# Cross-attention of a two-block transformer layer: its scores and its weighted values as three fp32r products of rounded parts and remainders instead of one fp32 product

## The reference, cut to what matters

```python
def cross_attention(xn, memn, w_q, w_kv, w_o):
    q = (xn @ w_q).reshape(b, s, 4, 256)
    k, v = jnp.split(memn @ w_kv, 2, axis=-1)        # reshaped to 4 heads of 256
    scores = jnp.einsum('bqhd,bkhd->bhqk', q, k) * (256 ** -0.5)
    p = jax.nn.softmax(scores, axis=-1)
    o = jnp.einsum('bhqk,bkhd->bqhd', p, v).reshape(b, s, D_MODEL)
    return o @ w_o
```

## Time and profile before

| | |
|---|---|
| median of 3 runs | 2152.03 us (2150.19 to 2152.68) |
| span of the profiled execution, first to last instruction | 2149.0 us |
| PE busy | 2109.2 us, 98% of the span |
| DVE busy | 1218.3 us, 57% |
| ACT busy | 850.1 us, 40% |
| the query, attention and output stage | about 1670 to 1754 us of the span |

### The profile page before, as it was taken

How to read it: one execution, slowest core, us unless ns; L and a number is a source line. 1 busy time by engine, 2 the same in 40 slices (tenths; PEclk the granted TensorE clock), 3 DMA queues, 4 the chain that set the end, 5 groups by cost and what they waited for, 6 DMA issues and landing times. The chain is left out here.

```text
span 2149.0 us, 27234 instructions
## 1 busy us (share of the span) xinstructions
PE 2109.2 (98%) x10128; PEld 1709.0 (80%) x10128; DVE 1218.3 (57%) x1970; ACT 850.1 (40%) x1315; POOL 114.8 (5%) x117
## 2 busy tenths in 40 slices
PE   7999999999999999999999999999999999999998
PEld 7988888878777778878888887777777778888886
DVE  6886776755666445443333347778664454343443
ACT  7532222242344443342222236665775344232233
POOL 2000000022000000010000002000002000000001
PEclk9999999999999999999999999999999999999999
DMA  8655444534222224323333323112223212333332
GB/s 336 214 185 184 160 166 159 186 96 126 88 75 74 88 89 127 97 71 98 98 98 98 94 84 106 61 60 79 79 69 118 69 59 89 103 95 96 98 98 69
DMA packets 66777, 238.41 MB, mean 111 GB/s; under 512 B 7848, under 2 KB 10024, under 8 KB 65904
## 3 DMA queue, kind: packets, MB, share of 16 engines
q1 hardware_dynamic: 60768, 218.81, 31.7%
q0 software_dynamic: 3728, 16.08, 2.4%
q10 hardware_dynamic: 2176, 2.10, 0.3%
HBM read 230.12 MB, written 4.21 MB: 109 GB/s over the span
## 5 line engine op out<-in xcount | busy, mean ns | idle before, releaser
L2031 PE MATMUL bank<-hhi,whi 128*128 128x512 f32 x1504 | 595.0, 396 | 2.3 <-DVE wlo L1203 2.2
L2032 PE MATMUL bank<-hlo,whi 128*128 128x512 f32 x1504 | 586.0, 390 | 0.0
L2033 PE MATMUL bank<-hhi,wlo 128*128 128x512 f32 x1504 | 585.8, 389 | 0.0
L1203 DVE TENSOR_TENSOR wlo<-raw,whi 128x1024 fp32r<-128x1024 f32 (+1 forms) x352 | 428.7, 1218 | 273.1 <-ACT whi L595 270.5
L595 ACT ACTIVATE whi<-raw 128x1024 fp32r<-128x1024 f32 (+1 forms) x352 | 367.2, 1043 | 454.1 <-PE bank L2033 401.7
L2031 PE MATMUL bank<-ghi,whi 128*128 128x512 f32 (+1 forms) x936 | 358.8, 383 | 7.4 <-DVE glo L1212 4.4
L2032 PE MATMUL bank<-glo,whi 128*128 128x512 f32 (+1 forms) x936 | 355.2, 380 | 0.0
L2033 PE MATMUL bank<-ghi,wlo 128*128 128x512 f32 (+1 forms) x936 | 354.9, 379 | 0.0
L2031 PEld LDWEIGHTS bank<-hhi,whi 128*128 128x128 f32 x1504 | 282.4, 188 | 67.1 <-issue 6.2
L2033 PEld LDWEIGHTS bank<-hhi,wlo 128*128 128x128 f32 x1504 | 282.3, 188 | 60.1
L2032 PEld LDWEIGHTS bank<-hlo,whi 128*128 128x128 f32 x1504 | 282.6, 188 | 56.8 <-issue 0.7
(11 more groups left out here) (302 smaller groups left out, 1929.6 us busy)
## 6 DMA issues: line engine op xcount, KB each, us to landing
raw<-w SPq DMA_DIRECT2D x389, 512.0 KB, 3.6
work<-w SPq DMA_DIRECT2D x12, 512.0 KB, 11.2
raw<-w SPq DMA_DIRECT2D x16, 384.0 KB, 3.1
gated_in<-gated_in POOLq DMA_DIRECT2D x40, 64.0 KB, 1.9
gated_in<-w SPq DMA_DIRECT2D x4, 512.0 KB, 9.9
xT<-x_t POOLq DMA_DIRECT2D x1, 2048.0 KB, 12.0
kv_hbm<-work POOLq DMA_DIRECT2D x2, 1024.0 KB, 4.8
work<-w POOLq DMA_DIRECT2D x4, 512.0 KB, 5.3
```

The lines of the kernel that those rows point to most:

```text
L1203: nc.vector.tensor_tensor(wlo[v % 2][:, 0:kc * P], raw[u % 4][:, 0:kc * P], whi[v % 2][:, 0:kc * P].bitcast(F32), ALU.subtract).then_inc(w ...
L2031: nc.tensor.matmul(dst, wh[:, ws], hi[:, c, :], start=c == 0, stop=False)
L2032: nc.tensor.matmul(dst, wh[:, ws], lo[:, c, :], start=False, stop=False)
L2033: ins = nc.tensor.matmul(dst, wl[:, ws], hi[:, c, :], start=False, stop=c == kc - 1)
```

## The change

Scores and values each become three fp32r products. The rounded parts are made on ACT and the remainders on DVE, for the keys (`xk_hi`, `xk_lo`), the values (`xv_hi`, `xv_lo`), the queries (into `ghi`, `glo`, one chunk at each c from 1 to 8) and the transposed probabilities (`xp_hi` by the copy that was there, `xp_lo` by two new DVE subtractions). The remainders of keys and values are written in place over the values they come from. PE waits for `xq_split`, `kv_split` and `xp_split` instead of `evac`, `kv_in` and `turned_out`.

```diff
--- before.py
+++ after.py
@@ -142,6 +142,13 @@
         def sb(name, shape, dt=F32):
             return ctx.enter_context(nc.sbuf_tensor(name, shape, dt))
 
+        def next_at():
+            return -(-nc.sbuf_base // 32) * 32
+
+        def rounded(name, shape, base, at_=0):
+
+            return nc.alloc_sbuf_tensor_at(name, [P, *shape], F32R, offset=base + 4 * at_)[:]
+
         def sem(name):
             return ctx.enter_context(nc.semaphore(name))
 
@@ -179,12 +186,17 @@
         square = [sb(f"square{i}", [P, S]) for i in range(2)]
         square_sum = sb("square_sum", [P, S])
         rstd = sb("rstd", [P, S])
-        normed = [sb(f"normed{i}", [P, S]) for i in range(2)]
+        normed_at = []
+        normed = []
+        for i in range(2):
+            normed_at.append(next_at())
+            normed.append(sb(f"normed{i}", [P, S]))
         gated_in = sb("gated_in", [P, 4 * S])
         gate_in = [gated_in[:, i * S:(i + 1) * S] for i in range(2)]
         opnd = [gated_in[:, (2 + i) * S:(3 + i) * S] for i in range(2)]
 
         WORK = 16100
+        work_at = next_at()
         work = sb("work", [P, WORK])
         at = [0]
 
@@ -250,6 +262,10 @@
         xq = place(DC, S)
         x_prob = [place(4, 2 * P) for _ in range(2)]
         x_probT = place(2, S)
+        xk_hi, xk_lo = (rounded(n, (DC, MEM), work_at, i * S) for n, i in (("xk_hi", 0), ("xk_lo", 4)))
+        xv_hi, xv_lo = (rounded(n, (2, D), work_at, i * S) for n, i in (("xv_hi", 26), ("xv_lo", 8)))
+        xp_hi = rounded("xp_hi", (2, S), work_at, 24 * S)
+        xp_lo = [rounded(f"xp_lo{kb}", (S,), normed_at[kb]) for kb in range(2)]
         at[0] = 25 * S
         memT = place(DC, MEM)
         x_vT = [place(MEM) for _ in range(2)]
@@ -323,6 +339,8 @@
         fsq_done, fsq_added, fsum_done, fr_ln, fr_done = (
             sem("fsq_done"), sem("fsq_added"), sem("fsum_done"), sem("fr_ln"), sem("fr_done"))
         unit_in = sem("unit_in")
+        kv_hi, kv_split = sem("kv_hi"), sem("kv_split")
+        xq_hi, xq_split, xp_split = sem("xq_hi"), sem("xq_split"), sem("xp_split")
         half_done, half_in, half_sq, half_sum, half_ln, half_root = (
             sem("half_done"), sem("half_in"), sem("half_sq"), sem("half_sum"), sem("half_ln"), sem("half_root"))
         out_v, stored = sem("out_v"), sem("stored")
@@ -1126,16 +1144,26 @@
                     norm_square(N_XATTN, c - 1)
             scaled_hi(N_XATTN, DC - 1)
             norm_square(N_XATTN, DC - 1)
+            def kv_rounded(src, dst):
+                nc.scalar.activation(dst, src, ACT.Copy).then_inc(kv_hi, 1)
+
             for c in range(DC + 4):
                 v = V_XQ + c
                 if c <= DC:
                     split_next(v)
                 if c == 0:
                     stats(N_XATTN)
+                    act.wait_ge(kv_in, 32)
+                    kv_rounded(xk, xk_hi)
+                if c == 1:
+                    kv_rounded(xv, xv_hi)
+                if 1 <= c <= DC:
+                    act.wait_ge(evac[(v - 1) % 2], (v - 1) // 2 + 1)
+                    nc.scalar.activation(ghi[:, c - 1, :], xq[:, c - 1, :], ACT.Copy).then_inc(xq_hi, 1)
                 if c >= 2 and c % 2 == 0 and c < DC + 2:
                     step_exp(16 + c // 2 - 1, x_prob, 0, False)
                 if c >= 3 and c % 2 == 1 and c < DC + 3:
-                    step_turned(16 + (c - 3) // 2, x_probT, range(2))
+                    step_turned(16 + (c - 3) // 2, xp_hi, range(2))
                 if c >= 5 and c % 2 == 1:
                     act.wait_ge(pv_out, 16 + (c - 5) // 2 + 1)
                     for e in range(2):
@@ -1946,6 +1974,23 @@
                 residual(V_WO2 + c, c)
             scaled_lo(N_XATTN, DC - 1)
 
+            def kv_remainder(k, src, hi, lo):
+                dve.wait_ge(kv_hi, k + 1)
+                nc.vector.tensor_tensor(lo, src, hi.bitcast(F32), ALU.subtract).then_inc(kv_split, 1)
+
+            def query_remainder(c):
+
+                dve.wait_ge(xq_hi, c + 1)
+                nc.vector.tensor_tensor(glo[:, c, :], xq[:, c, :], ghi[:, c, :].bitcast(F32),
+                                        ALU.subtract).then_inc(xq_split, 1)
+
+            def prob_remainder(hh):
+
+                dve.wait_ge(turned_out, 16 + hh + 1)
+                for kb in range(2):
+                    ins = nc.vector.tensor_tensor(xp_lo[kb], bank[4 + kb][:], xp_hi[:, kb, :].bitcast(F32), ALU.subtract)
+                ins.then_inc(xp_split, 1)
+
             def x_output(hh):
                 dve.wait_ge(pv_done, 16 + hh + 1)
                 for e in range(2):
@@ -1958,12 +2003,20 @@
                     dve.wait_ge(rstd_done, N_XATTN + 1)
                     dve.wait_ge(unit_done, v + 1)
                     nc.vector.tensor_tensor(xq[:, c, :], bank[v % 2][:], rstd[:], ALU.mult).then_inc(evac[v % 2], 1)
+                    if c == 0:
+                        kv_remainder(0, xk, xk_hi, xk_lo)
+                    if c == 2:
+                        kv_remainder(1, xv, xv_hi, xv_lo)
+                if 1 <= c <= DC:
+                    query_remainder(c - 1)
                 if c >= 2 and c % 2 == 0 and c < DC + 2:
                     softmax_first(16 + c // 2 - 1, x_prob, 0, False, XATTN_SCALE)
                 if c == DC:
                     split_next(V_XO)
                 if c >= 2 and c % 2 == 0 and c < DC + 2:
                     softmax_last(16 + c // 2 - 1, x_prob, 0, False)
+                if c >= 3 and c % 2 == 1 and c < DC + 3:
+                    prob_remainder((c - 3) // 2)
                 if c >= 5 and c % 2 == 1:
                     x_output((c - 5) // 2)
                     for e in range(2):
@@ -2529,31 +2582,36 @@
                 if 0 < c < DC:
                     unit(V_XQ + c, H)
                 if c == 2:
-                    pe.wait_ge(kv_in, 32)
+                    pe.wait_ge(kv_split, 1)
+                if c == 4:
+                    pe.wait_ge(kv_split, 2)
                 if c >= 2 and c % 2 == 0 and c < DC + 2:
                     hh = c // 2 - 1
-                    v = V_XQ + c - 1
-                    pe.wait_ge(evac[v % 2], v // 2 + 1)
-                    pe.wait_ge(evac[(v - 1) % 2], (v - 1) // 2 + 1)
+                    pe.wait_ge(xq_split, 2 * hh + 2)
                     pe.wait_ge(masked, 2 * (16 + hh))
                     for n in range(NB):
+                        dst, t = bank[2 + n // 2][:, (n % 2) * 2 * P:(n % 2 + 1) * 2 * P], slice(n * P, (n + 1) * P)
                         for e in range(2):
-                            ins = nc.tensor.matmul(bank[2 + n // 2][:, (n % 2) * 2 * P:(n % 2 + 1) * 2 * P],
-                                                   xq[:, 2 * hh + e, n * P:(n + 1) * P], xk[:, 2 * hh + e, :],
-                                                   start=e == 0, stop=e == 1)
+                            d = 2 * hh + e
+                            nc.tensor.matmul(dst, ghi[:, d, t], xk_hi[:, d, :], start=e == 0, stop=False)
+                            nc.tensor.matmul(dst, glo[:, d, t], xk_hi[:, d, :], start=False, stop=False)
+                            ins = nc.tensor.matmul(dst, ghi[:, d, t], xk_lo[:, d, :], start=False, stop=e == 1)
                     ins.then_inc(score_done, 1)
                 if c >= 3 and c % 2 == 1 and c < DC + 3:
+                    pe.wait_ge(xp_split, (c - 3) // 2)
                     turn_probs(16 + (c - 3) // 2, x_prob, range(2))
                 if c == DC + 1:
                     unit_part(V_XO + 1, G, 2, 4, first=(op_ready, J_XO))
                 if c >= 4 and c % 2 == 0:
                     hh = c // 2 - 2
-                    pe.wait_ge(turned_out, 16 + hh + 1)
+                    pe.wait_ge(xp_split, hh + 1)
                     pe.wait_ge(pv_out, 16 + hh)
                     for e in range(2):
+                        d, dst = slice((2 * hh + e) * P, (2 * hh + e + 1) * P), bank[6 + e][:]
                         for kb in range(2):
-                            ins = nc.tensor.matmul(bank[6 + e][:], xv[:, kb, (2 * hh + e) * P:(2 * hh + e + 1) * P],
-                                                   x_probT[:, kb, :], start=kb == 0, stop=kb == 1)
+                            nc.tensor.matmul(dst, xv_hi[:, kb, d], xp_hi[:, kb, :], start=kb == 0, stop=False)
+                            nc.tensor.matmul(dst, xv_hi[:, kb, d], xp_lo[kb], start=False, stop=False)
+                            ins = nc.tensor.matmul(dst, xv_lo[:, kb, d], xp_hi[:, kb, :], start=False, stop=kb == 1)
                     ins.then_inc(pv_done, 1)
                 if c == DC:
                     unit_part(V_XO, G, 0, 4, first=(op_ready, J_XO))
```

## The result

The changed kernel takes 2172.34 us (median of 4 runs, 2169.26 to 2173.36), the kernel before 2152.11 on the same chip (4 runs). The ratio is 1.0093, with a 95% interval of 1.0081 to 1.0105: 0.9% slower, 20.2 us. It was run a second time unchanged, in the first set of the experiments, with 2171.66 beside 2151.48.

What follows compares the result with a forecast made beforehand. PE, busy 98% of the span and in fixed order, bounds the kernel. New waits of 18.0 us less 5.2 spared, plus 4.8 for three clock falls, add 17.6 us to 2152.03: 2169.6 us, range 2162 to 2175.

Steps and rivals of the forecast that it cites:

- step 8: Scores of head 3: no query unit left before them, late remainder of query chunk 7; wait 7.3 us, net loss 7.2.
- steps 0 and 1, keys: Query unit 2 waits for wlo, made only after DVE's subtraction of the keys: wait 0.7 us, with the start 0.8.
- step 2, scores of head 0: Scores wait for query chunk 1's remainder, behind the values' subtraction on DVE: 3.8 us, with the start 3.9.
- step 4: Scores of head 1 wait for a query remainder, without the values' subtraction ahead: with the start 1.7 us.
- step 6: Scores of head 2 wait as probabilities' remainders and output copies make DVE late: 3.0 us, with the start 3.1.
- step 10, values of head 3: Last values wait for two DVE subtractions after ACT's copy: 1.3 us added.
- spared by the products: Scores and values of four heads: three fp32r products save 0.59 and 0.70 us per head, 5.2 us in all.
- falls of the clock: Behind waits of 3.8, 3.0 and 7.3 us the granted clock halves, 1.6 us each, 4.8 us; chance 0.47.
- Rival 1: Clock holds wholly or partly: no fall 2164.8 us, one 2166.4, two 2168.0; chance 0.08 none, 0.31 one or two.
- Rival 2: Queues of steps 5 and 7 don't pile up; each remainder costs only its own latency: 2154.9 us; chance 0.04.
- Rival 3: Faster: PE never waits for a remainder, 2146.8 us; a gain needs new waits together below 5.2 us; chance 0.03.
- Rival 4: A 256-column fp32r product costs more here, at worst 0.216 us: 9.2 us more, 2178.8 us; chance 0.06.

Runs made afterwards that it cites:

- no_remainders: Changed kernel without DVE's new subtractions, all three products taking rounded parts only, ACT's last two query roundings in step 7 (only its time is of use): 2146.04 us, 0.9974.
- filler: Changed kernel plus 28 unused fp32r products of 512 columns on PE in the wait before head 3's scores: 2168.9 us, 1.0079.
- early_query: Changed kernel with DVE making each query chunk's remainder ahead of its wait for the next unit, and the values' remainder a step earlier: 2166.41 us, 1.0064.
- reordered: All the change's work, ACT and DVE reordered: keys/values split ahead of the stage, queries in their own step, output copies before probabilities' remainders: 2149.73 us, 0.9992.
- reordered_head3_fp32: The reordered kernel with head 3's scores and values as single fp32 products, last quarter of keys and values not split: 2148.11 us, 0.9985.

## Why the prediction was right, and where its terms were off

The direction, the time (2169.6 against 2172.34, inside 2162 to 2175) and the mechanism held: queued remainders, above all at step 8. The places of the clock's falls were in part luck. Its terms against the profile after, waits before PE's start:

| term | forecast | measured |
|---|---|---|
| steps 0 and 1, keys | 0.7 | 0.5 |
| step 2, scores of head 0 | 3.8 | 3.7 |
| step 4 | 1.6 | 1.5 |
| step 6 | 3.0 | 2.8 |
| step 8 | 7.3 | 7.1 |
| step 10, values of head 3 | 1.4 | 2.4 |
| spared by the products | 5.2 | 5.1 (`no_remainders`: 4.5 and the wait of 0.6) |
| falls of the clock | 3, 4.8 us | 3, 5.3 us (4, 6.4 us in the second profile) |
| stage | +17.6 | +18.5 (+19.3 in the second) |

- **Prices.** The extended values for the long operations held: the keys' and values' roundings took 1.90 and 1.91 us, their remainders 2.29 and 2.28. The scores' products start 0.12 us apart at the full clock.
- **The steps 0 to 8.** Each wait came 0.1 to 0.25 us below its forecast. The list of what is ahead of a remainder in the two queues was enough for that. The 3 us that the upper end had for waits of several engines in turn were not needed. The 0.7 us for the longer bound of the long operations should have been 0.5 (0.20 and 0.16 in front of unit 2, 0.16 in front of the first scores), which moves nothing.
- **Step 10 was mis-sized.** I counted ACT's copy and two subtractions. The values of head 3 also wait for `pv_out`, and the output copies of head 2 now stand behind those subtractions: 2.4 us. The same shift I had counted at step 6 I forgot here. In the trace PE's releaser is the copy, not the remainder:

```profile
1762.24 1.29 DVE L1991 TENSOR_TENSOR xp_lo<-bank,xp_hi 128x512 fp32r<-128x512 f32 x2 [2.57 <-ACT xp_hi L805]
1763.44 1.28 DVE L1997 COPY work<-bank 128x512 f32<-128x512 f32 x2
...
1764.87 0.47 PE L2612 MATMUL bank<-xp_hi,xv_hi 128*128 128x512 f32 x1 [2.41 <-DVE work L1997]
```

- **The clock.** Three falls, but not those I named: waits of 3.7 and 7.1 us had one, that of 2.8 us had none in the first profile and one in the second and in `filler`, that of 2.4 us had one in both and none in `filler`, and that of 2.2 us in `early_query` had one. The fall that I named for step 6 didn't come in the first profile, and one that I hadn't named came at step 10, so the count of three was right by luck. The fall of step 8 cost 1.9 us and not 1.6, since it was twice as long and half hidden in the wait. The sum was right to 0.5 us by such offsets. The Trainium skill (TensorE: Matmul & The Clock Gate, Part 1, What's actually happening) says that the number of slow products at a kernel's start varies from run to run of one kernel. The traces agree for the start: the first slow stretch ends at 28.6 us in the first profile of the changed kernel and at 26.6 in the second (see below). The two profiles of the changed kernel show the same inside the stage, of which the page doesn't speak: three stretches in one and four in the other.
- **The four passes.** By the Trainium skill's rule of four passes (FP8 and Floating Point Precision, TensorE Precision Notes) the prediction estimated 6.9 us spared. `no_remainders` shows 4.5 and a wait of 0.6, so 5.1: the rows were the better guide.
- **The frame.** The medians differ by 20.2 us where I had 17.6. Of the 2.7 us between forecast and time, 0.9 lie in the stage by the first profile (18.5) and 1.7 by the second (19.3). The rest is not in the stage. Ahead of it the two profiles of the changed kernel differ by 2.3 us (see below), and no term of the sum stands for that. The 3.0 us that I laid around the span were not what lies around it: in all profiles of the changed kernels the profiled run is 1.8 to 2.2 us above its span, so the first profile was of an execution about a microsecond faster than the median of before. That moves nothing in the forecast, which is the median before plus the growth of the stage.
- **Rivals.** Rival 1 (a fall fewer) described neither profile. Rival 2 did not describe the changed kernel; `reordered`, which removes the queues, came out better than it (2149.73 against 2154.9), since only two latencies are left there. Rival 3 needed less than 5.2 us of new waits: `reordered` has 2.5, `reordered_head3_fp32` none, and both gained what that says. Rival 4 fell with `no_remainders`.

**The part ahead of the stage.** It holds no changed instruction, yet the stage began at 1668.6 to 1673.0 us in the twelve profiles. By the column of the granted clock this is not the clock: the stretches at 0.50 ahead of the stage cost 6.8 us in the profile of before and in the first after alike. But in the first microseconds of a profile the column reads 1.00 while the products go at the lower rate. Two windows, before and then after, both with products of 256 columns:

```profile
26.00:27.00 1.00, 1.00 (x11) 1.00 (x10) 1.00 (x2) 0.98 (x2) 0.00 (x0) 1.00 1.25 528
...
24.00:25.00 1.00, 1.00 (x7) 1.00 (x6) 0.97 (x3) 0.00 (x0) 0.00 (x0) 1.00 0.80 336
```

Both read 1.00, with eleven products in one and seven in the other; in the second they start 0.21 us apart. By this distance the first slow stretch ends at 18.5 us in the profile of before and at 28.6 in the first after. Before the first of these products, at 14.1 and 13.2 us, nothing shows the clock; if the stretch is counted from the span's start, it makes 32.1 and 42.3 us at the lower clock together with the later ones up to the stage. Over the twelve profiles this sum goes with the start of the stage (their correlation is 0.95): the three with the least (28.7 to 32.1 us: `no_remainders`, `reordered_head3_fp32` and before) begin it at 1668.6 to 1669.2, the three with the most (42.0 to 42.3: the first after, `early_query` and `filler`) at 1672.4 to 1673.0. So most of the 3.8 us is very likely the clock at the kernel's start. It is read from twelve profiles and not from an experiment.

**What stays open.** Which wait is followed by a fall, and what ends the first slow stretch earlier or later.

## What to carry to other kernels

When a product is replaced by parts that another engine must prepare, the saving is that of the products only where the preparation has work of the waiting engine to hide behind; list for each consumer everything that stands ahead of its operand in the queues of both preparing engines, and what was behind the new work before (here the output copies), since that becomes late too. Put the preparation of an operand right behind its making, and large constant operands into an earlier stage: that order alone was worth 22 us here, the new products 5. Where the last consumer has nothing to hide behind, leave it in the old form.

## What was not expected of the hardware

- Extra work on the waiting engine can shorten a kernel. With 28 idle products in a 7 us wait the granted clock stood at 1.00 at the next start, where the changed kernel had 0.50 in both profiles, and the time was about 3 us less (2168.9 against 2172.34 and 2171.66). The next fall stayed away too, which may be chance.
- A fall can come while PE stands, and lasts over its start: from 1745.5 to 1752.4, with PE starting at 1748.62. Products then run at half rate from their first one (0.21 us apart instead of 0.12), whereas behind the 3.7 us wait ten products ran at full rate before the clock fell.
- The shortest wait with a fall behind it in these stages was 2.2 us (`early_query`), and the earlier trace rows have one behind 1.77. None followed the wait of 1.5 us in the two profiles of the changed kernel, nor that of 1.4 us in the two of `reordered`.
- The column of the granted clock can read 1.00 where products run at half rate: so it does from 14.1 to 18.5 us in the profile before and from 13.2 to 28.6 us in the first after, where products of 256 columns start 0.21 us apart.
